# Second attention of a two-block transformer kernel: query roots in the exponential, rotations two chunks back, value projection last, transposes in front of the gathers

## The reference

```python
def rms_norm(x, g):
    xf = x.astype(jnp.float32)
    return (xf * lax.rsqrt(jnp.mean(jnp.square(xf), axis=-1, keepdims=True) + RMS_EPS) * g).astype(x.dtype)

def apply_rope_2(x, cos, sin):
    x1, x2 = jnp.split(x, 2, axis=-1)
    out = jnp.concatenate([x1 * cos - x2 * sin, x2 * cos + x1 * sin], axis=-1)
    return out.astype(x.dtype)

def attend(q, k, v):
    b_, h_, tq, hd = q.shape
    qg = q.reshape(b_, N_KV_HEADS, h_ // N_KV_HEADS, tq, hd)
    s = jnp.einsum('bkgqd,bktd->bkgqt', qg, k, preferred_element_type=jnp.float32) * (hd ** -0.5)
    p = jax.nn.softmax(s, axis=-1)
    o = jnp.einsum('bkgqt,bktd->bkgqd', p.astype(v.dtype), v)
    return o.reshape(b_, h_, tq, hd)

def gqa_mix(h_lat, h_ctx, w_qkv, q_norm_g, k_norm_g, w_o, cos, sin, with_ctx_out):
    kv_c = h_ctx @ w_qkv[:, Q_DIM:]
    k_c = rms_norm(split_heads(kv_c[..., :KV_DIM], N_KV_HEADS), k_norm_g)
    v_c = split_heads(kv_c[..., KV_DIM:], N_KV_HEADS)
    qkv = h_lat @ w_qkv
    q_l = apply_rope_2(rms_norm(split_heads(qkv[..., :Q_DIM], N_HEADS), q_norm_g), cos, sin)
    k_l = apply_rope_2(rms_norm(split_heads(qkv[..., Q_DIM:Q_DIM + KV_DIM], N_KV_HEADS), k_norm_g), cos, sin)
    v_l = split_heads(qkv[..., Q_DIM + KV_DIM:], N_KV_HEADS)
    k_all = jnp.concatenate([k_c, k_l], axis=2)
    v_all = jnp.concatenate([v_c, v_l], axis=2)
    y_lat = merge_heads(block_attend(q_l, k_all, v_all)) @ w_o
    ...
```

## Time and profile before

| | us |
|---|---|
| three timed runs, median (lowest, highest) | 2569.63 (2568.29, 2571.73) |
| profiled execution, whole | 2564.72 |
| span of that execution in the profile | 2562.9 |
| TensorE busy in the span | 2461.3 (96%) |
| VectorE busy | 1854.6 (72%) |
| ScalarE busy | 1107.6 (43%) |
| mean granted clock of TensorE | 0.987 of full speed |
| stretch of the second attention, 2230.27 to 2321.15 | 90.88 |

### The profile page before, as it was taken

How to read it: one execution, slowest core, us unless ns; L and a number is a source line. 1 busy time by engine, 2 the same in 40 slices (tenths; PEclk the granted TensorE clock), 3 DMA queues, 4 the chain that set the end, 5 groups by cost and what they waited for, 6 DMA issues and landing times.

```text
span 2562.9 us, 39610 instructions
## 1 busy us (share of the span) xinstructions
PE 2461.3 (96%) x15670; PEld 2234.7 (87%) x15670; DVE 1854.6 (72%) x3605; ACT 1107.6 (43%) x1658; POOL 0.2 (0%) x4
## 2 busy tenths in 40 slices
PE   4999999999999999999999999999999999998998
PEld 3998989999999888788888998888998888877998
DVE  7878988878878736768787669896785444676655
ACT  3444565444463324634232652232642322645444
POOL 0000000000000000000000000000000000000000
PEclk8999999999999999999999999999999999999999
DMA  8886766758867531654443256675373333212653
GB/s 314 304 268 221 255 216 228 259 194 270 292 203 224 179 99 59 214 160 129 139 147 121 87 190 209 193 236 198 95 259 125 114 107 96 83 58 75 198 191 105
DMA packets 161961, 455.80 MB, mean 178 GB/s; under 512 B 17776, under 2 KB 21360, under 8 KB 161776
## 3 DMA queue, kind: packets, MB, share of 16 engines
q1 hardware_dynamic: 161776, 453.26, 54.2%
HBM read 452.14 MB, written 1.05 MB: 177 GB/s over the span
## 4 chain that ended last, share of the span: by engine, by line
PE 77%; DVE 5%; ACT 2%; issue 1%; DMA 1%; ACTq 0%; DVEq 0%; SPq 0%
PE PS L1189 24%; PE PS L1190 24%; PE PS L1191 24%; DVE own L1678 1%; PE PS L1216 1%; PE PS L1343 1%; PE PS L1214 1%; DVE X L1659 1%; ACT own L1408 1%; PE PS L1389 1%; PE PS L1372 0%; DMA SCR<-in_ma 0%; ACT Uh L1469 0%; ACT NT L1473 0%; PE PS L1317 0%
## 5 line engine op out<-in xcount | busy, mean ns | idle before, releaser
L1189 PE MATMUL PS<-Uh,own 128*128 128x256 f32 (+1 forms) x2072 | 656.1, 317 | 41.5 <-DVE Ul L1759 21.3
L1190 PE MATMUL PS<-Ul,own 128*128 128x256 f32 (+1 forms) x2072 | 645.2, 311 | 0.0
L1191 PE MATMUL PS<-Uh,own 128*128 128x256 f32 (+1 forms) x2072 | 645.1, 311 | 0.0
L1408 ACT ACTIVATE own<-raw 128x1024 fp32r<-128x1024 f32 x429 | 448.2, 1054 | 374.3 <-PE PS L1191 305.8
L1678 DVE TENSOR_TENSOR own<-raw,own 128x1024 fp32r<-128x1024 f32 x429 | 520.1, 1219 | 70.3 <-ACT own L1408 70.1
L1189 PEld LDWEIGHTS PS<-Uh,own 128*128 128x128 f32 x2072 | 398.9, 193 | 70.6 <-issue 31.8
L1190 PEld LDWEIGHTS PS<-Ul,own 128*128 128x128 f32 x2072 | 400.0, 193 | 19.5 <-issue 0.2
L1191 PEld LDWEIGHTS PS<-Uh,own 128*128 128x128 f32 x2072 | 399.7, 193 | 19.7
L1189 PE MATMUL PS<-Hh,own 128*128 128x256 f32 (+1 forms) x1096 | 347.7, 317 | 1.0 <-DVE own L1678 0.6
L1190 PE MATMUL PS<-Hl,own 128*128 128x256 f32 (+1 forms) x1096 | 343.2, 313 | 0.0
L1191 PE MATMUL PS<-Hh,own 128*128 128x256 f32 (+1 forms) x1096 | 343.2, 313 | 0.0
(11 more groups left out here) (216 smaller groups left out, 3883.9 us busy)
## 6 DMA issues: line engine op xcount, KB each, us to landing
MODS<-in_mm SPq DMA_DIRECT2D x168, 256.0 KB, 3.5
SCR<-in_mm SPq DMA_DIRECT2D x136, 256.0 KB, 3.7
raw<-in_f0i SPq DMA_DIRECT2D x68, 512.0 KB, 4.2
raw<-in_f1i SPq DMA_DIRECT2D x56, 512.0 KB, 3.6
raw<-in_f2i SPq DMA_DIRECT2D x56, 512.0 KB, 3.6
SCR<-in_ma SPq DMA_DIRECT2D x88, 256.0 KB, 5.5
raw<-in_w1i SPq DMA_DIRECT2D x44, 512.0 KB, 4.8
raw<-in_w2i SPq DMA_DIRECT2D x44, 512.0 KB, 4.6
```

The lines of the kernel that those rows point to most:

```text
L1189: e.matmul(o, ll, rh, start=start, stop=False)
L1190: e.matmul(o, lh, rl, start=False, stop=False)
L1191: return e.matmul(o, lh, rh, start=False, stop=stop)
L1408: e.activation(parts(w.n)[0], raw[:, w.n % RING, :], ACT.Copy).then_inc(s["whi"].tell(w.n), 1)
```

## The change

Four things are done in the second attention.

The queries are no longer normalized before the scores. Their gain `qn` goes into the ScalarE copy out of PSUM, the rotation follows, and the token's root factor, times 1/sqrt(128), becomes the scale of the Exp and a factor of the negated maximum, both as a column in place of a constant. `spread`, `headnorm` and their VectorE parts are left for the four key slots only.

A query's rotation stands two chunks behind its projection, with its squares. The roots of all eight queries are taken once the last squares are summed.

The latent value chunks stand behind the query chunks, and the scores 0 and 1 between the first and the second of them.

In a round the transposes of i-2 stand in front of the gather of i-3, and what ScalarE and VectorE do with a gather's output is a piece of its own, `take2`, for round i-4.

```diff
-    p.drain(p.wide("av", "av", 0, 4, (0, 1), "v2"))
...
+    def turn_head(slot):
+        p.put("rope2", f=slot, k=len(p.turned), bank=p.bank())
+        p.turned.append(slot)
+
+    def norm_head(slot, rope):
+
+        p.put("spread", f=slot)
+        p.later(1, lambda: p.put("headnorm", f=slot, bank=p.bank()))
+        if rope:
+            p.later(2, lambda: turn_head(slot))
 
     for t_ in range(8):
         heads(t_, t_, LAT)
-        if t_ == 0:
+        p.later(2, lambda t_=t_: turn_head(t_))
+        if t_ == 2:
             p.put("roots", f=8)
-        if 1 <= t_ < 5:
-            by_chunk(norm_head(8 + t_ - 1, t_ - 1, (t_ - 1) % 2 == 0))
-        if t_ == 6:
-            p.put("roots", f=0)
-            by_chunk(norm_head(0, 0, True))
-        if t_ == 7:
-            by_chunk(norm_head(1, 1, True))
+        if 2 <= t_ < 6:
+            norm_head(8 + t_ - 2, t_ % 2 == 0)
+    values = p.wide("av", "av", 0, 4, (0, 1), "v2")
+    next(values)
     p.flush()
+    p.put("roots", f=0)
     p.put("roots", f=4)
-    for f in norm_head(2, 2, True):
-        f()
-
-    n2, steps = 16, {}
-    for i in range(n2 + 3):
+
+    n2, gathers = 16, []
+    for i in range(n2 + 4):
         if i < n2:
             p.put("score2", k=i, bank=p.bank())
-        if i % 2 and i // 2 + 3 < 8:
-            steps[i // 2 + 3] = norm_head(i // 2 + 3, i // 2 + 3, True)
-        for h in sorted(steps):
-            steps[h].pop(0)()
-            if not steps[h]:
-                del steps[h]
+        if i == 1:
+            p.drain(values)
         if 1 <= i <= n2:
             p.put("weigh2", k=i - 1)
-        if i >= 3:
-            p.put("gather2", k=i - 3, bank=p.bank(), after=tuple(p.h_free[q, 0] for q in range(8)))
         if 2 <= i <= n2 + 1:
             p.put("turn2", k=i - 2, bank=p.bank())
+        if 3 <= i <= n2 + 2:
+            gathers.append(p.put("gather2", k=i - 3, bank=p.bank()))
+        if i >= 4:
+            p.put("take2", k=i - 4, bank=gathers[i - 4].bank, after=tuple(p.h_free[q, 0] for q in range(8)))
...
-                    e.activation(head_of(w.f), PS[:, b, lo:hi], ACT.Copy).then_inc(s["qk2_x"].tell(w.f), 1)
+                    if w.f < 8:
+                        on.wait_sem(s_vecs, 16)
+                        e.activation(head_of(w.f), PS[:, b, lo:hi], ACT.Copy, scale=vec("qn")).then_inc(
+                            s["qk2_x"].tell(w.f), 1)
+                    else:
+                        e.activation(head_of(w.f), PS[:, b, lo:hi], ACT.Copy).then_inc(s["qk2_x"].tell(w.f), 1)
...
-                    e.activation(P2[:, w.k % 3, :], PS[:, b, :], ACT.Exp, bias=sm[:, 0:1], scale=float(P) ** -0.5,
-                                 accum_out=sm[:, 1:2]).then_inc(s["prob2"].tell(w.k), 1)
+                    e.activation(P2[:, w.k % 3, :], PS[:, b, :], ACT.Exp, bias=sm[:, 0:1],
+                                 scale=inv_of(w.k // 2)[:, w.k % 2:w.k % 2 + 1], accum_out=sm[:, 1:2]).then_inc(s["prob2"].tell(w.k), 1)
...
-                elif w.what == "gather2":
+                elif w.what == "take2":
                     h, qt = w.k // 2, w.k % 2
...
-                    e.tensor_scalar(inv_of(w.f), PS[:, b, 0:2], 1.0 / P, 1e-6, ALU.mult, ALU.add).then_inc(
+                    mean = 1.0 if w.f < 8 else 1.0 / P
+                    e.tensor_scalar(inv_of(w.f), PS[:, b, 0:2], mean, mean * P * 1e-6, ALU.mult, ALU.add).then_inc(
...
-                    dst, g = head_of(w.f), NT[:, 0, w.f % 2, :]
+                    dst, g = head_of(w.f), NT[:, 1, w.k % 2, :]
...
-                    e.tensor_scalar(sm[:, 0:1], sm[:, 0:1], -float(P) ** -0.5, None, ALU.mult).then_inc(
-                        s["weight2"].tell(("max", w.k)), 1)
+                    on.wait_ge(s["root_inv"], w.k // 2 - w.k // 2 % 4)
+                    e.tensor_scalar(sm[:, 0:1], sm[:, 0:1], inv_of(w.k // 2)[:, w.k % 2:w.k % 2 + 1], -1.0, ALU.mult,
+                                    ALU.mult).then_inc(s["weight2"].tell(("max", w.k)), 1)
```

More of the change, by code:

```diff
@@ L168, in __init__ @@
         self.last = None
+        self.turned = []
     def put(self, what, **fields):
@@ L1359, in tensor @@
                     claim(w.bank)
-                    on.wait_ge(s["head_x"], w.f)
+                    if w.f < 8:
+                        on.wait_ge(s["qk2_x"], w.f)
+                    else:
+                        on.wait_ge(s["head_x"], w.f)
                     on.wait_sem(s_map, 16)
@@ L1962, in vector @@
                         on.wait_ge(s["matmul"], ("headnorm", f))
-                        if f < 8 or f % 2 == 0:
-                            on.wait_ge(s["roped2"], f)
                     e.tensor_tensor(NT[:, 0, w.f % 2, :].rearrange("p (t n) -> p t n", t=2),
@@ L1972, in vector @@
                     on.wait_ge(s["qk2_x"], w.f)
-                    e.scalar_tensor_tensor(out=dst, in0=dst, scalar=vec("qn" if w.f < 8 else "kn"), in1=PS[:, b, 0:S],
+                    e.scalar_tensor_tensor(out=dst, in0=dst, scalar=vec("kn"), in1=PS[:, b, 0:S],
                                            op0=ALU.mult, op1=ALU.mult).then_inc(s["head_x"].tell(w.f), 1)
@@ L1976, in vector @@
                 elif w.what == "rope2":
-                    dst, g = head_of(w.f), NT[:, 0, w.f % 2, :]
+                    dst, g = head_of(w.f), NT[:, 1, w.k % 2, :]
                     on.wait_ge(s["matmul"], (w.id, 0))
+                    if w.k >= 2:
+                        on.wait_ge(s["roped2"], plan.turned[w.k - 2])
                     e.tensor_tensor(g, PS[:, b, 0:S], sin2, ALU.mult).then_inc(s["roped2"].tell((w.f, "sin")), 1)
```

## The result

| | before | after |
|---|---|---|
| timed beside each other (6 runs each), median us | 2568.32 (2566.37 to 2571.73) | 2559.90 (2559.19 to 2564.80) |
| ratio after/before, 95% interval | | 0.9971 [0.9961, 0.9981] |
| profiled execution, whole | 2564.72 | 2559.84 |
| stretch of the second attention | 90.88 | 84.54 |

The change makes the kernel faster by 0.29%: 7.4 us by the ratio, 4.9 to 10.0 by its interval. The forecast was 5.8 us less and 2563.8 us, with a range of 2558 to 2568.5. In the profiled executions the edited stretch is 6.34 us shorter. The windows of after have it whole, then its loop (fifth row maximum to the sixteenth), its tail, and two rows of five microseconds, the first with the end of its first scores (2269.28 to 2271.16) in it and the second, its least busy, around its first transposes; columns as in the earlier trace rows.

What follows compares the result with a forecast made beforehand. TensorE was taken to bound the old kernel, VectorE and ScalarE the new loop. 37.0 + 12.0 + 30.3 + 5.8 = 85.1 us against 90.88; 5.8 off the 2569.63 median gave 2563.8 us, range 2558 to 2568.5, inner 2561.5 to 2566.

Steps and rivals of the forecast that it cites:

- Piece A: Second attention from the first squares matmul to the start of query 7's rotation: 37.0 us.
- 13 extras: Rotations and squares-to-squares additions beside nine chunks before the last rotation: 0.44 us each, with 3.32 per chunk.
- wait for the key roots: TensorE's one remaining wait before the last rotation, as key roots are taken right before the first spread: 0.99 us.
- Piece B: From the start of rotation 7 to the fifth row maximum: 12.0 us, including a 1.5 us TensorE wait before the first transposes.
- Piece C: The loop, eleven rounds from the fifth to the sixteenth row maximum: 2.75 us a round, 30.3 us.
- the circle: VectorE and ScalarE waiting on each other from one row maximum to the next set the loop's round: 2.75 us.
- Piece D: The tail, from the sixteenth row maximum to the output projection: 5.8 us.
- The rule: Skill page's 1283 ns Exp table load plus about 1380 ns drain would delay the first Exp, adding some 0.2 us.
- the full gain: Rival: TensorE stays the loop's bound at 2.19 us a round; 12.0 us less, 2557.6 us; chance 6%.
- The short clock loss: Rival: clock falls for a few us after the value projection, adding about 2.4 us before the fifth maximum; 2566.2; 12%.
- the sustained one: Rival: idle TensorE holds the clock at 1.2 GHz in the loop, 4.4 us a round; 2582 us; chance 6%.
- The grown waits: Rival: waits before the fifth maximum and the loop's round grow together, 2.7 less gain; 2566.5 us; chance 12%.

Runs made afterwards that it cites:

- weigh_first: Changed kernel with the first weighing put ahead of the second latent value chunk; stretch 83.94 us against 84.54, one run only.
- take_early: Changed kernel with output copy and its low part put before the transposes in each round; stretch 79.93 us, loop 25.29, ratio to before 0.9962.
- filler: Changed kernel with one unused 256-column matmul added before every gather; stretch 85.39 us, rounds still 2.73, ratio to before 0.9978.
- filler2: Changed kernel with two unused 256-column matmuls added before every gather; stretch 90.93 us, rounds 3.05, one run only.
- const_operands: Changed kernel with Exp scale and negation factor as constants again, leaving out the query root factor; stretch 82.37 us, rounds 2.58, one run only.
- old_round: Changed kernel with the old order inside a round (gather and its copies, then transposes); stretch 85.24 us, ratio to before 0.9975.
- roots_only: Changed kernel with value chunks first and old round order, keeping query roots in the Exp and early rotations; stretch 85.51 us, ratio to before 0.9971.
- after_again: Changed kernel, unchanged, profiled and timed once more; 2561.89 us beside 2567.54 for the kernel before, ratio 0.9976, stretch 84.60.

## Why the prediction was right

By its own pieces, forecast and measured in the profile of after:

| | forecast | measured |
|---|---|---|
| A, to rotation 7 (2231.84 to 2268.76) | 37.0 | 36.92 |
| B, to the fifth maximum (2280.60) | 12.0 | 11.84 |
| C, eleven rounds (2310.61) | 30.3 | 30.01 |
| D, to the output projection (2316.38) | 5.8 | 5.77 |
| sum | 85.1 | 84.54 |

Piece A: counting 9 chunks and 13 extras by two old distances came within 0.1 us. The wait for the key roots was 0.84, not 0.99, and the work 36.08, not 35.97, so two small misses cancel. That wait is the only one above 0.5 us there, and no query chunk waits for VectorE.

Piece B: the order of queues decided it, as forecast. First maximum at 2.03 (2.07), second Exp at 3.80 (3.90), weighing done at 7.48 (7.57), transposes at 7.62 (7.63), a wait of 1.49 (1.5). weigh_first confirms that the weight's two copies are its cause.

Piece C: all five steps of the circle hold to 0.03 us; the copy of the transposes counts 0.47 instead of 0.50, and with it a round is 2.73 instead of 2.75, which over eleven rounds is most of the 0.3 us by which C was too long. That the circle is the bound was argued from the order then; take_early (order), filler (TensorE's slack), filler2 (its 2.19) and const_operands (the two columns) have shown it since.

Piece D: the old tail's 8.0 us come back with the old order (8.16 in old_round), so the gain there belongs to the transposes in front.

The rule: the load ends at 2270.72, and the first Exp starts exactly 1.00 us later, right when the negation (2271.47, 0.22 long) lets it go. The Trainium skill (ScalarE: Activation LUTs, What ACT_TABLE_LOAD costs) adds a drain of some 1380 ns to the load. The trace does not agree: ahead of the load the last square root ends 0.02 us before it, and even if all of the 1.00 behind it were drain, it would be less than the page says, and piece B was shorter than forecast, not 0.2 longer.

The rivals: the full gain needed rounds of 2.19; TensorE would have allowed them (filler2), the circle did not. The short clock loss and the sustained one both fell: 1.00 in all of the loop and from 2275 to 2280, behind the first scores, with 3.50 of 5 us busy; in roots_only, from 2275 to 2280 as well, with 3.54. The grown waits fell too; every wait was as forecast or smaller.

The absolute time was 3.9 us too high, and outside the prediction's own inner range of 2561.5 to 2566; it lies nearer to the full gain's 2557.6. So the whole time alone would not have told the two apart: that the forecast holds is known from the pieces, above all from rounds of 2.73 and not 2.19. 0.6 of it is the sum, 1.3 the base (2569.63 in the three runs shown, 2568.32 beside the runs of after), and the 2.0 left is the difference between 8.4 us by medians and 6.3 in the stretch. after_again has 5.7, so this can be scatter; both intervals (4.9 to 10.0 and 3.1 to 9.0 us) hold 6.3.

## What to carry to other kernels

Where two engines hand work to each other within their queues, add up one turn from start to start before trusting that a third engine is the bound; the turn, not the busy share, tells what a saved matmul is worth. Put the short instruction that releases the other engine in front of the long one that doesn't: here that was worth 4.7 us in eleven rounds, three quarters of what the whole change gained in its stretch. A saving that is right in itself can also be given back by another part of the same change, so each part is to be timed alone.

## What the runs showed of the hardware

A window that reads 97% busy for TensorE had room for 0.43 us more work in each 2.73, since the ends of its records are modelled; only added work or the distance of starts tells. A column in place of a constant costs 0.09 us in an Exp of 512 elements and 0.06 in a negation of one (as far as const_operands can tell them apart). And the clock can drop to 0.66 for some microseconds at a place where, in another execution, it doesn't; in the executions with such drops the work around them took 2 to 5 us longer, about as much as this change is worth, so a kernel is better compared by its stretch than by one whole time.
